# Attention heads of a two-block model: rotary squares joined on Pool, token sums of a head in one run in the value bank

## The reference, cut to what matters

```python
q = (rmsnorm_2(c_q, q_norm_g) @ w_uq).reshape(B, S, N_HEADS, QK_DIM)       # 8 heads, 128 + 64
kv = (rmsnorm_2(c_kv, kv_norm_g) @ w_ukv).reshape(B, S, N_HEADS, QK_NOPE + V_DIM)
k = jnp.concatenate([k_nope, k_pe_h], axis=-1)
q = rmsnorm_2(q, qk_q_g)          # per token and head, over 192 features
k = rmsnorm_2(k, qk_k_g)
...                               # rotary turn of the last 64 features
for s0 in range(0, S, Q_BLOCK):   # blocks of 128 queries, causal
    s = einsum(q[:, s0:e], k[:, :e]) * scale
    p = softmax(where(mask, s, -inf))
    outs.append(einsum(p, v[:, :e]))
```

## Time and profile before

| what | value |
|---|---|
| runs of the kernel | 3897.42, 3903.8 and 3903.86 us; median 3903.8 |
| span of the profiled execution | 3896.1 us |
| between that span and the three runs | 1.3 to 7.8 us |
| PE busy | 3563.3 us, 91% of the span |
| DVE, ACT, Pool busy | 41%, 23%, 30% |
| the attention stage | from 2056.5 to 2530.6 us of the span |

### The profile page before, as it was taken

One profiled execution on the slowest core, in us unless ns is written; L12 is line 12 of the kernel. 1 busy time (PEld: TensorE's weight loads), 2 busy tenths in 40 slices (PEclk: granted clock), 3 DMA queues, 4 the chain that ended last, 5 costly groups with the idle time before them and its releaser, 6 DMA issues. The chain is left out here.

```text
span 3896.1 us, 50558 instructions
## 1 busy us (share of the span) xinstructions
PE 3563.3 (91%) x21562; PEld 2677.6 (69%) x21562; DVE 1608.8 (41%) x2302; ACT 887.3 (23%) x1528; POOL 1174.1 (30%) x781
## 2 busy tenths in 40 slices
PE   5999987999689999999978999999999997899995
PEld 3788876888577888878766777678788883333332
DVE  4433546666647777733142333310752323111112
ACT  3223323232231101011122333310630113111110
POOL 3122226777433444433520000033343231122220
PEclk7989998999899999999987998999999997999998
DMA  5223346445241111121110000022111318899997
GB/s 232 70 100 127 121 146 166 127 106 125 66 130 49 49 49 49 49 86 48 67 33 22 6 12 6 2 62 60 38 44 49 125 51 345 351 386 371 375 388 285
DMA packets 324487, 484.39 MB, mean 124 GB/s; under 512 B 27256, under 2 KB 275984, under 8 KB 306984
## 3 DMA queue, kind: packets, MB, share of 16 engines
q1 hardware_dynamic: 299240, 443.85, 32.8%
q0 software_dynamic: 18432, 23.12, 1.7%
q10 hardware_dynamic: 6592, 14.19, 1.0%
HBM read 533.04 MB, written 75.96 MB: 156 GB/s over the span
## 5 line engine op out<-in xcount | busy, mean ns | idle before, releaser
L1870 PE MATMUL ps_ff<-ffn_in_high,ff_parts 128*128 128x512 f32 x1376 | 425.5, 390 | 6.6 <-PEq L98 6.6
L2455 POOL CAST w_br_high<-acc 128x1024 fp32r<-128x1024 f32 x56 | 72.2, 1289 | 935.3 <-DMA acc<-in_w_in_dram 527.2
L1870 PEld LDWEIGHTS ps_ff<-ffn_in_high,ff_parts 128*128 128x128 f32 x1376 | 259.5, 189 | 60.9 <-issue 7.0
L1870 PE MATMUL ps_ff<-ffn_in_low,ff_parts 128*128 128x512 f32 x688 | 268.6, 390 | 0.0
L1974 DVE SCALAR_TENSOR_TENSOR acc<-grid,vec,acc 128x1024 f32<-128x1024 f32 x154 | 256.3, 1664 | 5.5
L2858 PE MATMUL mo_ps_h<-mo_w,mo_xT 128*64 128x512 f32 x1024 | 229.7, 601 | 2.4 <-DVE mo_xT L3047 2.4
L3053 DVE TENSOR_TENSOR mo_g<-mo_s,mo_ps_h 128x256 f32<-128x256 f32 x48 | 20.2, 421 | 501.7 <-ACT mo_s L2927 501.7
L1870 PE MATMUL ps_ff<-hidden_high,ff_parts 128*128 128x512 f32 x704 | 219.4, 392 | 7.3 <-DVE hidden_low L1961 7.3
L1856 POOL CAST ff_parts<-acc 128x1024 fp32r<-128x1024 f32 (+1 forms) x66 | 83.9, 1271 | 430.7 <-PE ps_ff L1870 409.8
L2513 PE MATMUL ps_br<-u_high,w_br_high 128*128 128x512 f32 x512 | 203.6, 398 | 9.7 <-POOL w_br_low L2457 9.0
L2513 PE MATMUL ps_br<-u_low,w_br_high 128*128 128x512 f32 x512 | 200.2, 391 | 0.0
(11 more groups left out here) (631 smaller groups left out, 8020.3 us busy)
## 6 DMA issues: line engine op xcount, KB each, us to landing
mo_w<-in_exp_w_dram SPq DMA_DIRECT2D x63, 2048.0 KB, 13.5
mo_w<-in_exp_w_dram SPq DMA_DIRECT2D x63, 1024.0 KB, 9.2
tokp<-tok_scratch SPq DMA_DIRECT2D x20, 896.0 KB, 11.3
pj_w_mod<-in_w_ada_columns_dram SPq DMA_DIRECT2D x32, 512.0 KB, 4.8
acc<-in_w_in_dram SPq DMA_DIRECT2D x32, 512.0 KB, 4.0
DT<-rows_scratch SPq DMA_DIRECT2D x19, 768.0 KB, 9.0
feat<-feat_scratch SPq DMA_DIRECT2D x19, 768.0 KB, 9.9
acc<-in_ffn_w_gate_dram SPq DMA_DIRECT2D x22, 512.0 KB, 3.9
```

Source lines behind the costliest of these rows:

```text
L1870: last = mm(ps[t % sets][:, c, 0:width], rounded(a[:, k, :]), rounded(x[:, k, at:at + width]), start=(k == 0 and j == 0), stop=(k == n - 1 ...
L2455: nc.gpsimd.tensor_copy(rounded(high[:, :, :]), raw[t % 2][:, :, :]).then_inc(high_taken, 1)
```

## The change

The unit `sums` leaves the list of units, which has 10 entries now; the spread units are 8 and 9. Four things take its place:

- Pool adds the 64 rotary rows of squares into the first 64 rows of `sq[:, 0]` once both are there, and signals `joined`. The 8 products of 64 rows are gone.
- PE makes the remaining 16 products in four calls of `sums` in one run, in step 4 ahead of the second value unit, and writes them to columns 128 to 143 of the value bank `po` rather than to a `pj` bank. Before the run it waits until the output of step u - 2 has been copied out of `po`; before the value products of step 3 it waits for `sums_taken`. For head 0 the run is behind both value units, ahead of the spread.
- DVE takes the sums in a function `take_sums` in step 4, behind the maximum of step 5 and ahead of the copy of the output. It reads `po`.
- ACT takes the root in step 4, behind the exponential of step 5, rather than in step 3.

`v` 0 is alone in step 3, and `v` 1 stays in step 4. SP's wait is on unit 8 of 10 instead of 9 of 11, which is the second value unit as before.

```diff
-HEAD_UNITS = [("q", 0), ("q", 1), ("q_rope", 0), ("q_rope", 1), ("k", 0), ("k", 1), ("v", 0), ("sums", 0), ("v", 1), ("spread", 0), ("spread", 1)]
-UNITS_AT = {0: (0, 1), 1: (2, 3), 2: (4, 5), 3: (6, 7), 4: (8,), 5: (9, 10)}
+HEAD_UNITS = [("q", 0), ("q", 1), ("q_rope", 0), ("q_rope", 1), ("k", 0), ("k", 1), ("v", 0), ("v", 1), ("spread", 0), ("spread", 1)]
+UNITS_AT = {0: (0, 1), 1: (2, 3), 2: (4, 5), 3: (6,), 4: (7,), 5: (8, 9)}
+SUMS_AT = {4: ((7, 0, 0), (7, 0, 4), (7, 2, 0), (7, 2, 4))}
+SPREAD = HEAD_UNITS.index(("spread", 0))
...
-                        sp.wait_ge(unit_done, UPH * (h - 2) + 9)
+                        sp.wait_ge(unit_done, UPH * (h - 2) + 8)
...
-                    elif kind == "sums":
-                        pe.wait_ge(squared, 3 * (h + 1))
-                        for t in range(NX):
-                            at = slice(t * P, (t + 1) * P)
-                            nc.tensor.matmul(out[:, t:t + 1], sq[:, 0, at], S.ones[:, 0:1], start=True, stop=False)
-                            nc.tensor.matmul(out[:, t:t + 1], sq[0:ROPE, 1, at], S.ones[0:ROPE, 0:1], start=False, stop=True)
-                            last = nc.tensor.matmul(out[:, NX + t:NX + t + 1], sq[:, 2, at], S.ones[:, 0:1], start=True, stop=True)
...
+                def sums(h, i, first):
+                    if i == 0:
+                        pe.wait_ge(joined, h + 1)
+                    else:
+                        pe.wait_ge(squared, 3 * (h + 1))
+                    for t in range(first, first + 4):
+                        at = P + (NX if i else 0) + t
+                        last = nc.tensor.matmul(po[:, at:at + 1], sq[:, i, t * P:(t + 1) * P], S.ones[:, 0:1], start=True, stop=True)
+                    if i and first:
+                        last.then_inc(summed, 1)
...
                 for j in range(UPH):
+                    if j == SPREAD:
+                        for i, first in ((0, 0), (0, 4), (2, 0), (2, 4)):
+                            sums(0, i, first)
                     head_unit(0, j)
...
+                    if following:
+                        if at in SUMS_AT:
+                            pe.wait_ge(o_copied, u - 1)
+                        for j in UNITS_AT.get(at, ()):
+                            for unit, i, first in SUMS_AT.get(at, ()):
+                                if unit == j:
+                                    sums(h + 1, i, first)
+                            head_unit(h + 1, j)
...
                     if u >= 1:
+                        if following and at == 4:
+                            pe.wait_ge(sums_taken, h + 2)
                         values(u - 1)
...
+                def root(h):
+                    act.wait_ge(sums_taken, h + 1)
+                    nc.scalar.activation(norm[:, h % 2, :], norm[:, h % 2, :], ACT.Sqrt).then_inc(rooted, 1)
...
+                    if u % NX == 4 and h + 1 < NH:
+                        root(h + 1)
...
+            @block.gpsimd
+            def _(pool):
+                for h in range(NH):
+                    pool.wait_ge(squared, 3 * h + 2)
+                    nc.gpsimd.tensor_tensor(sq[0:ROPE, 0, :], sq[0:ROPE, 0, :], sq[0:ROPE, 1, :], ALU.add).then_inc(joined, 1)
...
+                def take_sums(h):
+                    dve.wait_ge(summed, h + 1)
+                    stt(norm[:, h % 2, :], po[:, P:P + 2 * NX], 1.0 / QK, tok[:, :], ALU.mult, ALU.add).then_inc(sums_taken, 1)
...
                     if u + 1 < U:
                         maximum(u + 1)
+                    if u % NX == 4 and u < U and h + 1 < NH:
+                        take_sums(h + 1)
                     if u >= 1:
                         w_h, w_b = units[u - 1]
                         dve.wait_ge(pv_done, u)
```

More of the change, by code:

```diff
@@ L2132, in mla_heads @@
     with ExitStack() as ctx, stage(
-            nc, "w_in0", "w_in1", "unit_done", "free0", "free1", "rope_squared", "squared", "sums_taken", "rooted", "inverted", "head_ready", "scores_done",
+            nc, "w_in0", "w_in1", "unit_done", "free0", "free1", "rope_squared", "squared", "joined", "summed", "sums_taken", "rooted", "inverted", "head_ready", "scores_done",
             "max_done", "exp_done", "probs_done", "turned", "turned_out", "pv_done", "o_copied", "mask_ready", "chain") as sems:
@@ L2136, in mla_heads @@
         unit_done = sems[2]
-        (rope_squared, squared, sums_taken, rooted, inverted, head_ready, scores_done, max_done, exp_done, probs_done, turned, turned_out,
+        (rope_squared, squared, joined, summed, sums_taken, rooted, inverted, head_ready, scores_done, max_done, exp_done, probs_done, turned, turned_out,
          pv_done, o_copied, mask_ready, chain) = sems[5:]
@@ L2231, in _ @@
                 for u in range(U + 1):
+                    at, following = u % NX, u < U and units[u][0] + 1 < NH
+                    h = units[u][0] if u < U else NH
                     if u + 1 < U:
                         scores(u + 1)
+                    if following:
[6 more added lines that the diff above has]
+                            head_unit(h + 1, j)
+                            for unit, i, first in SUMS_AT.get(at, ()):
+                                if unit == -j:
+                                    sums(h + 1, i, first)
                     if u < U:
-                        h, _b = units[u]
-                        for j in UNITS_AT.get(u % NX, ()) if h + 1 < NH else ():
-                            head_unit(h + 1, j)
                         turn(u)
                     if u >= 1:
+                        if following and at == 4:
+                            pe.wait_ge(sums_taken, h + 2)
                         values(u - 1)
@@ L2262, in head_unit @@
                             act.sem_inc(squared, 1)
-                    elif kind == "sums":
-                        act.wait_ge(sums_taken, h + 1)
-                        nc.scalar.activation(norm[:, h % 2, :], norm[:, h % 2, :], ACT.Sqrt).then_inc(rooted, 1)
+                def root(h):
+                    act.wait_ge(sums_taken, h + 1)
+                    nc.scalar.activation(norm[:, h % 2, :], norm[:, h % 2, :], ACT.Sqrt).then_inc(rooted, 1)
                 def exponential(u):
@@ L2276, in _ @@
                 for j in range(UPH):
+                    if j == SPREAD:
+                        root(0)
                     head_unit(0, j)
@@ L2308, in head_unit @@
                         nc.vector.tensor_copy(v[h % 2][:, 4 * c:4 * c + 4, :].rearrange("p t c -> p (t c)"), src[:, :]).then_inc(done, 1)
[L2309 to L2313, removed]
                     elif kind == "spread":
@@ L2337, in _ @@
                 for j in range(UPH):
+                    if j == SPREAD:
+                        take_sums(0)
+                        inverse(0)
                     head_unit(0, j)
-                    if HEAD_UNITS[j][0] == "sums":
-                        inverse(0)
                 maximum(0)
```

## The result

The changed kernel takes 3857.31 us (median of 4 runs, 3851.55 to 3862.83) against 3900.61 us for the kernel before: ratio 0.9894, 95% interval 0.9872 to 0.9917, which is 41 us less (32 to 50 us). The prediction was 3855 us. The profiled execution has a span of 3849.8 us, 46.3 us less than before.

A forecast was written before the change was run, and what follows sets the result against it. The prediction took PE to bound the attention stage, partly at half clock. Steady heads 43 us (52.0 less 9 for falls) plus head 0's 6 us made 49 us, off a median of 3903.8: 3855 us, range 3838 to 3877.

The forecast's parts named there:

- PE sets the pace: Attention stage, steady part: PE busy 422.2 of 441.9 us, so time taken from it is gained while DVE and ACT stay ahead.
- The run of 16: Token sums of each head: 16 products at 0.24 us take 3.8 us; bounds 3.4 and 7.2 us.
- The steady part without falls at the sums: Seven steady heads: 91.2 - 7 x (3.8 + 1.8) = 52.0 us gained before pricing clock falls.
- The falls: PE clock drops at the new sums: five in seven steady heads, 1.8 us each, 9 us lost.
- Rival (b): Sums: the 3.8 us run never costs the clock; 60 us gained, 3844 us; chance 15%.
- Rival (c): Sums: the clock falls in each head and stays low for 10.2 us; 3885 us; chance 12%.
- Head 0: Stage start-up: first scores come 6 us earlier, despite a new PE wait of 1.1 us.
- Pool, the two new waits, ACT's root: Pool's addition of about 2.4 us, waits for copied output and taken sums, and the moved root: all at nothing.
- The place of the run: Sums moved between block 2's scores and the second value unit: no gain of its own counted for steady heads.
- The sum: Whole kernel: 43 us steady plus 6 us head 0, 49 us gained, giving 3855 us.
- A clock of 0.95 or more: Sign in the changed profile: mean PE clock of the steady part at 0.95 or more.
- (e): Rival: Pool's sum and DVE hold each other up so PE waits; 3925 us at 12 us a sum; chance 3%.

The follow-up runs named there:

- e10: The e3 kernel with head 0's run in halves, and DVE in step 6 scaling the block before multiplying the second spread unit's keys; 3827.2 us, ratio 0.9806.
- e3: The changed kernel with its 16 products in four groups of four between dense units; 3840.2 us, ratio 0.9860.
- e2: The changed kernel without Pool's addition, all 24 products in the new place (move only); 3898.5 us, ratio 1.0004.
- e4: The changed kernel with each of the 16 products made twice, 32 in one run; 3905.0 us, ratio 1.002.
- e6: The changed kernel without Pool's addition, rotary squares left out of the query's sum, still 16 products; 3850.8 us, ratio 0.9877.
- e1: The kernel before with only Pool's addition, 16 products in the old place and bank; 3850.5 us, ratio 0.9885.
- e7: The changed kernel with the second value unit between the 8 query and 8 key products; 3839.1 us, ratio 0.9839.
- e5: e2 with 128 rows of key squares in place of each 64-row product, still 24 products; 3874.9 us, ratio 0.9939.
- e8: The changed kernel with the whole run behind the second value unit, rather than ahead of it; 3849.4 us, ratio 0.9865.

## Why the prediction was right, point by point

- **PE sets the pace: shown.** What PE lost, the stage lost: of a standstill cut by 1.43 us (e10) 1.35 us a head came through, and the same products grouped otherwise (e3) gave back the time at the half clock.
- **The run of 16: 3.8 us forecast, 3.54 measured.** The 0.24 us that I took was a step next to 64-row products; between 128-row products it is 0.221. The lower bound, 0.21, would have been nearer. This is 0.26 us a head, 2 us. The step into a 64-row product, too, is 0.29 us and not 0.31 (only the first, in the earlier trace rows, is 0.21).
- **The steady part without falls at the sums: 52.0 us forecast, 55.5 measured** (449.6 - 394.1, before against e3). Of the difference of 3.5 us, 1.8 is the shorter run, seven times, and 1.7 the fall of 3.4 us just behind the first scores, which the kernel before has and e3 has not.
- **The falls: the term that was mis-sized.** I took five in seven at 1.8 us, 9 us. There were six in seven, four of 3.4 us (a head 1.6 us longer) and two of 6.8 us (3.3 us longer): 13.0 us, the amount by which the changed kernel's steady heads are longer than those of e3, which lose no clock at the sums. With the 1.5 us from head 0's fall the steady part is 14.5 us longer. So 55.5 - 14.5 = 41.0 us in place of 43: the 52.0 was 3.5 us too small and the 9 us of falls 5.5 us too small, and the two errors partly cancel. My reading that a run of this length lies nearer to the stretches that seldom cost the clock was wrong. Rival (b), no fall, did not come with a run of this length; its state is reached when the run is split (e3), at 3840 us where I worked out 3844. Rival (c), about 10 us in each head, is what e2 and e4 show for longer runs (6.8 to 13.7 us).
- **Head 0: 6 us forecast, 5.7 measured.** The new wait of 1.2 us is there.
- **Pool, the two new waits, ACT's root: nothing forecast, nothing found** (e6, the list of waits).
- **The place of the run: priced at nothing for the steady heads; e2 shows nothing (1.0004).** The join alone (e1) is as fast as both together by the time of the launch.
- **The sum: 49 us forecast; 46.7 in the stage, 41 (32 to 50) by the ratio.** A clock of 0.95 or more came as stated, and the heads came 50 to 52 us apart but for one at 53.2. That the time came out 2 us from the forecast is partly luck: the forecast took a gain a few us too large from a median of 3903.8 us, and with one more run the median of the kernel before is 3900.6.
- **A sum of a rival.** In (e), an addition of 12 us would by its own terms give (12 - 2.1) x 8 - 49 = 30 us more than before, 3934 us and not 3925. It bears on the 3% only.

Left open: why the falls come in one head for 3.4 and in another for 6.8 us, and in one head not at all. Heads with the same instructions differ in it. The traces show that the fall shifts against the sums from head to head: it began 2.4, 2.9, 3.3, 3.7 and 4.0 us after the first sum in five successive heads of the kernel before, 57.6 us apart, and 4.3, 3.9, 3.5 and 3.1 us after it in the last four of the changed kernel, 51.6 us apart. So a head's instructions alone do not set it; but no experiment here held all else still and moved only the moment at which a head begins. The counts of falls are of one profiled execution of each kernel. Whether other data would change the clock was not tried either.

## What to carry to other kernels

A product with an output of one column is not nearly free: here it cost 0.22 us, as much as one of 128 columns, and in a long row it cost the clock of dense work behind it too. Count such products, and deal them out in groups of 1 to 2 us between dense products, which here took another 13 us from the steady heads (e3), a third of what the change itself had taken from the steady part. Fold a partial contraction (here 64 rows) into the operand of a full one on an idle engine, rather than adding it with a product of its own. When an edit has two parts, run each alone: here one carried the gain, and the other only became useful when it was used to split the run (e3, e7).

## What the runs showed of the hardware

A float32 product with an output of one column took 0.221 us at the full clock (16 in 3.54 us, the changed kernel). The value products with an output of 128 columns take as long: 16 instructions, which are 8 products, in 1.79 us.

A product of 64 rows between products of 128 rows was dearer than one of 128 rows: a token tile of three took 0.84 us with it and 0.67 us without (e2, e5), all at the full clock with one output column.

The clock fell as late as 0.7 us after the run of one-column products was over in the changed kernel (4.3 us after the first, the run being 3.54 us) and 1.3 us after it in e8 (4.8 us after the first of 3.49 us), so that it was the dense work behind that ran at half. In the steady heads, by the length that the run has at the full clock: runs of 7.1 and 6.8 us cost 6.8 to 13.7 us at the half clock, runs of 5.3 us 6.8 to 10.2, runs of 3.5 us 0 to 6.8, runs of 1.8 and 0.9 us between dense units none. A standstill of 1.89 us with transposes behind it was followed by 3.4 us at the half clock in one to three of the seven heads of each kernel that has it, 18 of 77 in all; one of 0.46 us (e10) in none of seven.

An addition of 64x1024 float32 values took 2.35 us on Pool, about as long as one of 128x1024 (2.40 us).
